# Three output units in place of two in the shared start of four matrix products

## The reference, cut to what matters

```
x = x + rmsnorm(m, norm_g[layer, 1])
f = conv_ffn(rmsnorm(x, norm_g[layer, 2]), ffn_w_in[layer], ...)   # entries "f0", "f1"
x = x + rmsnorm(f, norm_g[layer, 3])
...
down = rmsnorm(x, kv_norm_g) @ kv_w_down                           # entry "kvd"
c_q = rmsnorm(h @ q_w_down[j], q_norm_g[j])                        # "qd", behind "kvd"
...
u = rms_norm(h, norm_mix[l]); proj = u @ w_in[l]                   # entry "in"
```

## Time and profile before

| | us |
|---|---|
| runs of the kernel | 2282.17, 2272.46, 2279.74 |
| median | 2279.74 |
| the profiled execution, in full | 2276.96 |
| its span | 2275.2 |
| TensorE busy | 2155.8 (95%) |
| VectorE busy | 1299.6 (57%) |
| ScalarE busy | 907.5 (40%) |
| mean share of the 16 DMA engines busy with the dynamic queue | 23.8% |

### The profile page before, as it was taken

How to read it: one execution, slowest core, us unless ns; L and a number is a source line. 1 busy time by engine, 2 the same in 40 slices (tenths; PEclk the granted TensorE clock), 3 DMA queues, 4 the chain that set the end, 5 groups by cost and what they waited for, 6 DMA issues and landing times.

```text
span 2275.2 us, 36808 instructions
## 1 busy us (share of the span) xinstructions
PE 2155.8 (95%) x14590; PEld 1696.0 (75%) x14590; DVE 1299.6 (57%) x1948; ACT 907.5 (40%) x1453; POOL 113.8 (5%) x128
## 2 busy tenths in 40 slices
PE   4999999988999999899998999998999999999997
PEld 2866666676788888667776888886767887888886
DVE  4766777775654635676636635455755555434344
ACT  4764444434432323446644323233335444313222
POOL 0002222211000000100010000001000000000001
PEclk8999999989999999999999999999999999999999
DMA  3310010013232232111211333323211232333321
GB/s 126 97 44 24 15 26 18 25 39 130 74 102 90 95 102 83 56 52 32 66 59 53 104 98 97 98 85 100 66 50 42 78 112 84 101 97 98 102 83 65
DMA packets 53030, 168.94 MB, mean 74 GB/s; under 512 B 6920, under 2 KB 11144, under 8 KB 52768
## 3 DMA queue, kind: packets, MB, share of 16 engines
q1 hardware_dynamic: 52896, 167.07, 23.8%
HBM read 164.95 MB, written 2.10 MB: 73 GB/s over the span
## 4 chain that ended last, share of the span: by engine, by line
PE 88%; DVE 8%; ACT 2%; issue 1%; DMA 0%; SPq 0%; DVEq 0%; ACTq 0%
PE bank L1858 58%; PE bank L2359 3%; PE bank L1969 2%; PE bank L1900 2%; PE bank L1934 2%; PE bank L2253 2%; PE bank L1883 2%; PE bank L1986 2%; PE bank L2056 1%; PE bank L2068 1%; PE bank L2290 1%; PE bank L2272 1%; DVE rstd L1114 1%; PE bank L2369 1%; PE bank L2101 1%
## 5 line engine op out<-in xcount | busy, mean ns | idle before, releaser
L1108 DVE TENSOR_TENSOR w_lo<-w_raw,w_hi 128x1024 fp32r<-128x1024 f32 (+3 forms) x322 | 370.2, 1151 | 204.5 <-ACT w_hi L615 199.6
L1858 PE MATMUL bank<-a_hi,w_hi 128*128 128x512 f32 x1224 | 478.9, 391 | 0.0
L1858 PE MATMUL bank<-a_lo,w_hi 128*128 128x512 f32 x1224 | 476.3, 389 | 0.0
L1858 PE MATMUL bank<-a_hi,w_lo 128*128 128x512 f32 x1224 | 476.2, 389 | 0.0
L615 ACT ACTIVATE w_hi<-w_raw 128x1024 fp32r<-128x1024 f32 (+3 forms) x322 | 311.2, 969 | 215.9 <-PE bank L1858 202.4
L1858 PEld LDWEIGHTS bank<-a_hi,w_lo 128*128 128x128 f32 x1224 | 229.8, 188 | 49.0 <-issue 1.4
L1858 PEld LDWEIGHTS bank<-a_hi,w_hi 128*128 128x128 f32 x1224 | 229.7, 188 | 48.9 <-issue 1.4
L1858 PEld LDWEIGHTS bank<-a_lo,w_hi 128*128 128x128 f32 x1224 | 229.7, 188 | 47.8
L1858 PE MATMUL bank<-b_hi,w_hi 128*128 128x512 f32 x616 | 243.1, 395 | 15.0 <-DVE b_lo L1167 14.9
L1858 PE MATMUL bank<-b_hi,w_lo 128*128 128x512 f32 x616 | 240.6, 391 | 0.0
L1858 PE MATMUL bank<-b_lo,w_hi 128*128 128x512 f32 x616 | 240.5, 390 | 0.0
(11 more groups left out here) (335 smaller groups left out, 3359.3 us busy)
## 6 DMA issues: line engine op xcount, KB each, us to landing
w_raw<-in_f0gu SPq DMA_DIRECT2D x44, 512.0 KB, 3.6
w_raw<-in_f1gu SPq DMA_DIRECT2D x44, 512.0 KB, 3.6
w_raw<-in_f2gu SPq DMA_DIRECT2D x44, 512.0 KB, 3.6
w_raw<-in_f0dn SPq DMA_DIRECT2D x16, 512.0 KB, 3.6
w_raw<-in_f1dn SPq DMA_DIRECT2D x16, 512.0 KB, 3.6
w_raw<-in_f2dn SPq DMA_DIRECT2D x16, 512.0 KB, 3.6
w_raw<-in_kl SPq DMA_DIRECT2D x12, 512.0 KB, 3.6
w_raw<-in_in SPq DMA_DIRECT2D x10, 512.0 KB, 3.7
```

The source lines that it names most:

```text
L1108: dve.tensor_tensor(w_lo[r][:, 0:n, :], raw[r][:, 0:n, :], w_hi[r][:, 0:n, :].bitcast(F32), ALU.subtract).then_inc(w_split[r], 1)
L1858: mm = pe.matmul(bank[r][:, :], w[r][:, k, :], a[:, k, :], start=(k == 0 and n == 0), stop=(k == kt - 1 and n == 2))
```

## The change

One constant is changed. In each of the four entries unit 2 is computed tile by tile together with units 0 and 1, and no longer whole behind them.

```
-WIDE = 2
+WIDE = 3
 FIRST_AHEAD = ((), (4,), (), (5,))
```

## The result

The changed kernel is slower: 2291.26 us in the median of 4 runs (2289.13 to 2292.66) against 2277.34 us for the kernel before (4 runs, 2272.46 to 2282.17), ratio 1.0059 with a 95% interval of 1.0041 to 1.0076. So the loss is 11 to 14 us in the medians. Four executions in the record, of 2908 to 5509 us, are left out of every ratio as slow; the medians of e3, e5 and of the kernel before beside e5 to e8 count one each, which moves none by more than 0.2 us. The profiled execution took 2289.13 us with a span of 2287.3, 12.1 more than before.

What follows compares the result with a forecast made beforehand. TensorE, busy 95% of the span, was taken to bound the kernel, with no wait in the shared starts. Losses of 3.1 + 3.1 + 5.1 + 0 = 11.3 us gave 2288.3 or 2291.0; stated 2290, range 2281 to 2297.

Steps and rivals of the forecast that it cites:

- What bounds: Shared starts of the four entries: TensorE's pieces join with no wait, so moved matmuls fill nothing, gain 0.
- the prediction's own sign (less than 5): Shared starts: taking less than 5 us more each would show they had waits and the prediction was wrong.
- The rival of 16 us to win: Shared starts have room by weight-load share, so 16 us could be taken in: about 2264; chance 0.04.
- The delay of 4.76 us: Each entry: the last sum of squares runs 21 x 0.227 = 4.76 us later against everything following on TensorE.
- The feed-forwards: First gate/up pairs: unit 4 stalls 1.16 us and unit 5 1.82 more, with restart 3.1 us each.
- `in`: Last input projection's entry: the split of unit 4 stays covered with 1.3 us left, cost 0 us.
- `kvd`: MLA down-projection's entry: 3.5 us idle before `qd` plus 1.6 for the lower clock, 5.1 us in all.
- the queue behind `rstd`: VectorE: bank reads and weight splits queue behind the waiting reciprocal and move by 4.76 us with it.
- The clock: Half rate for 3.1 us behind the gap at `qd` loses 1.6 us; in the feed-forwards it stays up, 0.
- Sum: Whole kernel: 3.1 + 3.1 + 5.1 + 0 = 11.3 us slower, 0.5%, stated as 2290 us.
- Rival 2: Feed-forwards: VectorE and ScalarE catch up within the first pair, only `kvd` pays 3.9 to 5.1: about 2284; chance 0.15.
- rival 3: Clock also falls in the feed-forwards or stays low 6.4 us at `qd`: 13 to 16 us, about 2292 to 2296; chance 0.30.

Runs made afterwards that it cites:

- e3: The kernel before, with three units wide in the two feed-forward entries alone: 2283.72 us, ratio 1.0026.
- e5: The kernel before, with three units wide in all four entries and every sum of squares one tile earlier in TensorE's list: 2284.74 against 2281.02 us, ratio 1.0017.
- e8: The kernel before, with one unit wide in all four entries: 2283.21 against 2281.02 us, ratio 1.0003.
- e11: The changed kernel run again on another occasion, against the kernel before: 2289.76 against 2278.98 us, ratio 1.0045.
- e4: The kernel before, still two units wide, with only the last sum of squares put 21 matmuls later in each entry: 2289.43 us, ratio 1.0049.
- e1: The kernel before, with three units wide in the last input projection's entry alone: 2276.88 against 2277.05 us, ratio 0.9998.
- e2: The kernel before, with three units wide in the MLA down-projection's entry alone: 2282.96 us, ratio 1.0021.
- the parts: e1, e2 and e3 taken together, each against the kernel before: -0.2, +5.9 and +6.7 us in the medians, 12.4 together.
- e6: As e3, with the weight splits of units 4 and 5 one unit's body earlier on ScalarE and VectorE: 2288.6 against 2281.02 us, ratio 1.0032.
- e7: As e2, with 16 more matmuls into a bank nobody reads, behind the MLA down-projection's entry: ratio 1.0011 against the kernel before.

## Why the prediction was right

- *What bounds.* "There is no wait in it" held: the shared starts got longer by three matmuls per tile (5.2 to 5.6 us in the profile after), and e8 shows that there was no room for one unit, let alone three. In e11's profile `f0` got only 4.3 us longer, which by the prediction's own sign (less than 5) would speak for waits; but its later tiles take the same 2.9 us, and it is the first tile, at the lower clock, that is 0.9 us shorter than in the first profile. The rival of 16 us to win fell with it. Weight-load share had spoken for that rival; the spacing of starts was the better witness.
- *The delay of 4.76 us.* In the changed kernel the last sum starts at 586.20, and 33 matmuls of unit 2 (tile 7), units 0 and 1 (tile 7) and unit 3 are behind it. Unit 4 starts 9.79 us later; less its stall of 1.41 (the bracket's 1.25, and 0.16 by which a row of 0.39 outlasts its spacing of 0.227) that is 8.38, against 595.66 - 582.52 = 13.14 before: 4.76. e4 shows that this alone is the cause.
- *The feed-forwards.* 3.1 us each were forecast, as 1.2 before unit 4 and 1.8 before unit 5. The rows have 1.25 and 1.35; the stages lost 2.9 and 3.3, e3 6.7 for both. The idle time in a row is counted from the modelled end of the matmul before, so a start-to-start reading is the surer one: unit 4 to unit 5 is 603.06 - 595.99 = 7.07 us in place of 5.44, 1.63 more. With the 1.41 of unit 4 that is 3.04. The sum was right, its division slightly off.
- *`in`.* 0 forecast, -0.2 (e1) and +0.1 (stage) measured.
- *`kvd`.* 3.5 us of gap and 1.6 of clock were forecast, 5.1 in all; 5.9 (e2's medians), 5.4 (the stage in e2's and in e11's profile) and 6.7 (first profile) were measured. The delay and the queue behind `rstd` were right, two terms were small. The gap is 4.0, because the first matmul came at 976.33, 0.7 after the split ended at 974.40 + 1.23 = 975.63. The sum had stopped at the split and left out the read `down_kv` behind it, for which the same matmul waits (`bank_free0`) and which ends about 0.6 later. And the clock stayed down for 3.4 us in some executions and for 6.8 in others, where I had taken 3.1.
- *The clock.* That it would stay up in the feed-forwards held in all 16 gaps of 1.24 to 1.38 us there (changed kernel, e3, e4, e11). The row that it leaned on, the gap of 1.88 us, was a weak one: at the same place the clock did fall in e6 and e7.
- *Sum.* 11.3 us forecast; 13.9, 10.8, and 12.4 by the parts were measured. That the stated 2290 lies 1.3 from the measured 2291.26 is partly luck: the median it started from, 2279.74, came out 2.4 lower with the fourth run, and the loss 2.6 higher. The forecast lay close to the bound of 0.5%, and the measured ratios lie on both sides of it.
- *Rival 2* (covered in the feed-forwards) fell with e3, *rival 3* (more of the clock) holds half: not in the feed-forwards, but at `qd`.

## What to carry to other kernels

Before more work is put beside a producer, look whether the consumer waits at all: if the pieces of the chain join, there is nothing to fill, and the order of the work is all that can change. Then look for the one small result in that stretch on which later engines hang, here a sum of squares of 0.86 us, and keep as much of TensorE's work behind it as possible; the price of a delay is the delay less the smallest slack, and all later slacks have to be listed, not the next two alone. List for each of them everything that it waits for, the read that frees its bank too, and not only what the profile names. And look how a kernel's runs are spread before an effect of 0.2% is read from a median. In e8 the backlog that the lower clock left at the entry of `in` covered the producer's pace for the rest of it.

## What the runs showed of the hardware

A gap of TensorE of 1.99 us (e5) and gaps of 2.40 and 2.45 (e6) were each followed by 3.4 us at granted clock 0.50 (1.2 GHz); 16 gaps of 1.24 to 1.38 in the feed-forwards were not. One and the same gap of some 1.9 us in the attention was followed by 13 us at 0.50 in e6 and by 17 in e7, and by none in the eleven other traces. The gap of 4.0 us at `qd` was followed by 3.4 us at the lower level in e2 and e11; in the first profile of the changed kernel and in e4 the level was low for 6.8, of which the first 1.9 and 1.6 fell in the gap itself. Counted from the last sum of squares, the two profiles of the changed kernel differ by 0.8 us at this place. The first matmul of a unit came 0.05 to 0.25 us after the last VectorE operation that it waited for, in the feed-forwards and, with the bank read, at `qd`.
